# Dilated attention passes that read their tokens as stepped slices of an already transposed tile, in place of transposing raw tokens anew

## The chip, the cores and the metric

The kernel runs on one core of a Trainium2 chip. The metric is the device time of one execution in microseconds; the figure for a kernel is the median of its runs. TensorE multiplies and transposes, ScalarE (ACT), VectorE (DVE) and GpSimd (POOL) work elementwise, and SyncE (SP) issues most DMAs. A matmul of TensorE is preceded by a load of its stationary operand (a weight load, PEld in the profile).

## What is computed

Two groups of tokens, 512 (prompt) and 1024 (sample), each with 1024 features, go through two layers with shared weights. Layer 0 mixes with two kinds of attention, layer 1 with a windowed one, and a routed mixture of experts follows each. The change lies in the dilated half of layer 0's mixer:

```python
h = rms_norm(x, norm_mix[layer])
proj = h @ w_in                       # qa, ka, va (3 groups of 4 heads), qb, kb, vb
A_PATTERNS = ((128, 1), (512, 4), (2048, 16))       # (window, dilation)
for gi, (window, dil) in enumerate(A_PATTERNS):
    o, lse = dilated_window_attn(qa[:, :, gi], ka[:, :, gi], va[:, :, gi], window, dil)
    # to_sub: t.reshape(b, n, dilation, h, dh).transpose(0, 2, 1, 3, 4)
    # tokens of one residue modulo the dilation attend to each other in a band
```

So for dilation 4 and 16 the tokens of a tile of 128 are not neighbours: they are those of one residue modulo a step. The kernel uses steps (1, 1), (4, 4) and (4, 8) for (prompt, sample), and a mask for what is left of 16.

## The kernel before

Tokens are held in NT = 12 tiles of P = 128 (4 of prompt, 8 of sample). `attention_phase` (L390) is called three times in all: "b" (dense, 0 to about 684 us), "a" (dilated, about 684 to 1204 us) and "c" (layer 1). Between them stand `output_phase` and `expert_phase`, which the change does not touch.

For the projections the tokens lie transposed in SBUF, features on partitions and tokens as columns: `hTh` and `hTl`, [128, 8, 1536] of 4-byte values, a high and a low part whose sum is the value. `exact3` (L148) makes one product of three matmuls, high x high, high x low, low x high (L151 to L153). The stationary operand is the slice of 128 tokens, `hTh[:, k, tile_cols(p)]`, and the moving one 384 columns of weights. A projected tile p takes 8 blocks k x 3 = 24 matmuls into `psP`.

The norm is split: the token's 1/rms is not applied to the tokens, but later. `rt` holds the root for each token (applied to V in `evacuate`, L650), and `em` its mean square times EPS (used by `head_roots`, L608). Both are [128, 3, 12]: token within a tile, order (one for each pattern), tile.

Phase "a" runs 6 passes of 12 projected tiles (p = 0 to 71): passes 0 and 1 are pattern a1, 2 and 3 are a4, 4 and 5 are a16; the two passes of a pattern hold two heads' groups each. The order of all work is one list of events (`Work.banded_order`, L269), which every engine walks:
- "P" (p, half): `project`, 12 matmuls; after the second half ScalarE evacuates (`evacuate`, L641 to L650) and squares, GpSimd and VectorE norm and rotate.
- "T": TensorE turns q and k of tile p (L952, L955), ScalarE and VectorE write their high and low parts.
- "S", "R", "V": scores, turned probabilities and the weighted sum of attention, which follow the projection by LAG = 5 tiles. In V's order SP stores the output (L570), with two buffers `osb` in turn.
- "W": split of a quarter of the weights (L627 on ScalarE, L748 on VectorE), loaded by SP.
- "N" (n, half): half a tile of raw tokens. SP loads 256 KB (`load_x`, L524 to L528) with the tokens of the pattern's order (`token_rows`), TensorE transposes four blocks of 128x128 (`turn_x`, L923 to L929), ScalarE casts to `hTh` (L638) and squares `xb` for the mean square (L634), VectorE subtracts to `hTl` (L756), and GpSimd makes `em` and `rt` after the second half (`token_root`, L581 to L589).

`fresh` (L424) says which passes begin a new order of tokens. Phase "b" transposes all 12 tiles once in natural order, and pattern a1 uses them. For a4 and a16 `hTh` and `hTl` are overwritten in place: the 12 tiles "N" of a4 are taken one by one with the projected tiles p = 13 to 24, the 12 of a16 with p = 37 to 48. So the passes 0, 2, 4 and 5 are free of "N" but for their tile 0 in 2 and 4.

`psT` is one double buffer for the results of "N", "T" and "R"; a new one waits until the one before the last was copied out (`room_free`, L911).

Of the kernel before, what the change touches and what calls it, by code (L numbers as in the profile page):

```python
# [7 lines left out]
F32 = mybir.dt.float32  # L8
# [7 lines left out]
P = 128  # L16
SEQ, DEC_SEQ = 512, 1024
TOK = SEQ + DEC_SEQ
NT = TOK // P
# [20 lines left out]
STRIDES = {"b": (1, 1), "c": (1, 1), "a1": (1, 1), "a4": (4, 4), "a16": (4, 8)}  # L40
# [107 lines left out]
def exact3(eng, out, a, b, start, stop):  # L148

    (ah, al), (bh, bl) = a, b  # L150
    eng.matmul(out, ah, bh, start=start, stop=False)  # L151
    eng.matmul(out, ah, bl, start=False, stop=False)  # L152
    return eng.matmul(out, al, bh, start=False, stop=stop)  # L153
# [48 lines left out]
    return first, last - first, base + (first - t + 1) * P  # L202


def token_rows(rows, t, kind):

    g = t >= PT
    stride, first, n, u = STRIDES[kind][g], SEQ * g, (SEQ, DEC_SEQ)[g], t - PT * g
    r, part = divmod(u, n // stride // P)
    return rows[first:first + n].rearrange("(i r) c -> r i c", r=stride)[r, part * P:(part + 1) * P]  # L210


RING, LAG, HELD = 6, 5, 4
# [173 lines left out]
        return u % (self.nq // 2), self.units[u][2][k][0][0] * 3 * P  # L387


def attention_phase(nc, state, name, steps, hT, roots, x_rows, norm_gain, identity, masks, mask0, table, sink=None):  # L390

# [5 lines left out]

    ph = Phase(nc, state)  # L400
    hTh, hTl = hT
    rt, em = roots
    NS = len(steps)
    nq, nkv = steps[0]["nq"], steps[0]["nkv"]
    turns = steps[0]["w"].shape[0] - 1
    nh = nq + nkv
    NC = (nq + 2 * nkv) * HD
# [5 lines left out]
    N = turns * NS  # L413
# [3 lines left out]
    kblk = (pairs + single) * P  # L417
    TC = kblk + nkv * P
    OR = 4 if dense else 2
    XH = {"b": 4, "a": 2, "c": 3}[name]  # L420
    HC = D // 2
    SG = 2 if dense else nq
    order_of = [st["order"] for st in steps for _ in range(turns)]
    fresh = [(order_of[i - 1] if i else None if name != "a" else 0) != order_of[i] for i in range(N)]  # L424
    work = Work(steps, turns, fresh)
    units, groups, events, batch0 = work.units, work.groups, work.events, work.batch0
    UT = len(units)
# [10 lines left out]
    half = ph.sb("half", [P, nh])  # L438
    xb = ph.sb("xb", [P, XH, HC])
    ssx = ph.sb("ssx", [P, 2, 2])  # L440
# [30 lines left out]
    psP = ph.psum("psP", [P, 512])  # L471
# [3 lines left out]
    w_in = [ph.sem(f"w_in{x}") for x in range(RING)]  # L475
    x_in = [ph.sem(f"x_in{x}") for x in range(XH)]
    x_turned, x_high, x_low = ph.sem("x_turned"), ph.sem("x_high"), ph.sem("x_low")
    x_squared, rt_ready = ph.sem("x_squared"), ph.sem("rt_ready")
# [7 lines left out]
    pv_done, o_done, stored = ph.sem("pv_done"), ph.sem("o_done"), [ph.sem(f"stored{x}") for x in range(OR)]  # L486
    dve_order, pool_order, sink_ready = ph.sem("dve_order"), ph.sem("pool_order"), ph.sem("sink_ready")
    half_ready, tally = ph.sem("half_ready"), ph.sem("tally")
    NCONST = 1 + NS + (masks is not None) + (sink is not None)

    def place(p):
# [11 lines left out]
    def tile_cols(p):  # L503
        return slice(p % NT * P, (p % NT + 1) * P)
# [9 lines left out]
    with nc.Block() as block:  # L514

        @block.sync
        def _(sp):
            halves = 2 * len(work.norms)

            def load_x(x):  # L520
                if x >= halves:
                    return
                i, t = work.norms[x // 2]
                if x >= XH:  # L524

                    sp.wait_ge(x_squared, x - XH + 1)
                rows = token_rows(x_rows, t, work.kinds[i])
                sp.dma_start(xb[:, x % XH], rows[:, x % 2 * HC:(x % 2 + 1) * HC]).then_inc(x_in[x % XH], 16)  # L528

            def load_w(q):  # L530
                if q >= N * WQ:
                    return
                if q >= RING:

                    i, quarter = divmod(q - RING, WQ)
                    sp.wait_ge(projected, 2 * (i * NT + NT - 1) + quarter // 2 + 1)
                sp.dma_start(raw_quarter(q), weights(q)).then_inc(w_in[q % RING], 16)

            sp.dma_start(ident, identity).then_inc(ident_in, 16)
            if work.norms[0][0] == 0:  # L540
                load_x(0)
                load_x(1)
            sp.dma_start(gn[:, :], norm_gain).then_inc(gn_in, 16)
            load_w(0)
            load_w(1)
            for x in range(2 if work.norms[0][0] == 0 else 0, XH):
                load_x(x)
            load_w(2)
            load_w(3)
            for s, st in enumerate(steps):  # L550
                sp.dma_start(gains[:, s, :], st["gain"]).then_inc(const_in, 16)
            sp.dma_start(rope[:, :, :, :, :], table).then_inc(const_in, 16)
            if masks is not None:
                sp.dma_start(maskf[:, :], masks).then_inc(const_in, 16)
            if sink is not None:
                sp.dma_start(sinks[:, :], sink).then_inc(const_in, 16)
            ph.clear_previous(sp)
            load_w(4)
            load_w(5)
            for e in events:  # L560
                if e[0] == "N":
                    load_x(2 * e[1] + e[2] + XH)
                if e[0] == "P" and e[1] % NT == NT - 1:
                    for quarter in (0, 1):
                        load_w(e[1] // NT * WQ + RING + 2 * e[2] + quarter)
                if e[0] == "V":
                    for p in tile_done(e[1]):
                        s, turn, t = place(p)
                        sp.wait_ge(o_done, e[1] + 1)
                        sp.dma_start(steps[s]["out"](turn, t), osb[:, p % OR].rearrange("p h c -> p (h c)"))\  # L570
                          .then_inc(stored[p % OR], 16)
            for x in range(OR):
                sp.wait_ge(stored[x], 16 * (total // OR))
# [49 lines left out]
        def _(act):  # L623
# [17 lines left out]
            def evacuate(p):  # L641
                b, (s, _, t) = p % 2, place(p)
                if p >= 2:
                    act.wait_ge(gained, p - 1)
                n = [work.norm_of[i, t] for i in range(p // NT + 1) if (i, t) in work.norm_of]
                if n:
                    act.wait_ge(rt_ready, n[-1] + 1)
                act.wait_ge(projected, 2 * p + 2)
                act.copy(xr[:, b, :], psP[:, 0:nh * HD])
                act.mul(V[:, t, :], psP[:, nh * HD:NC], rt[:, steps[s]["order"], t:t + 1]).then_inc(evacuated, 1)  # L650
# [86 lines left out]
        def _(dve):  # L737
            chain = Chain(dve, dve_order)
            def constants():
                dve.wait_ge(const_in, 16 * NCONST)  # L740
                if sink is not None:
# [163 lines left out]
        def _(pe):  # L905
# [24 lines left out]

            def project(p, half):
                i, t = divmod(p, NT)
                if half == 0 and p:
                    pe.wait_ge(evacuated, p)
                n = [work.norm_of[j, t] for j in range(i + 1) if (j, t) in work.norm_of]
                if n:
                    pe.wait_ge(x_low, 2 * n[-1] + half + 1)
                for k in range(half * KD // 2, (half + 1) * KD // 2):
                    q = i * WQ + k // KW
                    if t == 0 and k % KW == 0:  # L940
                        pe.wait_ge(w_split, q + 1)
                    ins = exact3(pe, psP[:, 0:NC], (hTh[:, k, tile_cols(p)], hTl[:, k, tile_cols(p)]),
                                 (wh[:, q % RING, k % KW, :], wl[:, q % RING, k % KW, :]), k == 0, k == KD - 1)
                ins.then_inc(projected, 1)

# [757 lines left out]
def encoder(nc, a, stop=99):  # L1703
    dram = lambda name, shape: nc.dram_tensor(name, shape, F32, kind="Internal").ap()
    y_rows, x_rows = a["y"], a["x"]
# [11 lines left out]
    with ExitStack() as ctx:  # L1717
        state = {"n": 0, "old": [], "stack": None, "kept": ctx}
# [11 lines left out]
                    expert_phase(nc, state, a["w_gate"][layer], a["w_up"][layer], a["w_down"][layer], a["identity"],  # L1730
                                 lists, idx[:, :], gate[:, :], h_rows, y_rows)

        rt = ctx.enter_context(nc.sbuf_tensor("rt", [P, 3, NT], F32))
        em = ctx.enter_context(nc.sbuf_tensor("em", [P, 3, NT], F32))
        roots = (rt, em)
        with nc.sbuf_tensor("hTh", [P, KD, TOK], F32R) as hTh, nc.sbuf_tensor("hTl", [P, KD, TOK], F32R) as hTl:
            attention_phase(nc, state, "b",
                            [dict(kind="b", nq=B_NQ, nkv=1, order=0, w=a["w_b"], gain=a["gain_b"], out=by_tile(ob, B_NQ))],
                            (hTh, hTl), roots, x_rows, a["gain_mix"][0], a["identity"], None, 0, a["rope_axial"])
            attention_phase(nc, state, "a",  # L1740
                            [dict(kind=k, nq=2, nkv=2, order=s, w=a["w_a"][s], gain=a["gain_a"][s], out=by_residue(s, k))
                             for s, k in enumerate(("a1", "a4", "a16"))],
                            (hTh, hTl), roots, x_rows, a["gain_mix"][0], a["identity"], a["masks"][:, 3 * P:], 3 * P, a["rope_a"])
        moe(0, [(ob, A_OUT)], arec, a["w_out_ab"], x_rows)
        if stop <= 2:
            return
# [56 lines left out]
```

## Time and profile before

| | us |
|---|---|
| median of 3 runs | 4094.46 |
| lowest, highest | 4088.36, 4096.05 |
| profiled execution | 4093.49 |
| its span, first to last instruction | 4091.7 |

| engine | busy us | share of the span |
|---|---|---|
| TensorE, matmuls | 3819.6 | 93% |
| TensorE, weight loads | 3687.8 | 90% |
| VectorE | 2675.3 | 65% |
| ScalarE | 2138.2 | 52% |
| GpSimd | 860.1 | 21% |

The profile is of one execution. Matmuls are pipelined, so the duration of one (0.33 us for 384 columns) is longer than the distance between the starts of two in a row; the distance is what counts. The dilated phase is some 520 of the 4092 us. The granted clock of TensorE was at or near its full level of 2.4 GHz through nearly all of it (0.97 of full as a mean from 684 to 1204 us).

### The profile page before, as it was taken

Reading aid. Unit: us, or ns where it says so; the run is one execution under the profiler, and the core shown is the slowest. Engines: PE = TensorE matmul, PEld = TensorE weight load, DVE = VectorE, ACT = ScalarE, POOL = GpSimd, SP = SyncE. Lnnn points to the kernel's source line nnn. Section 1 sums busy time; section 2 is a strip of 40 time slices with the busy share of each in tenths; the row PEclk is TensorE's granted clock in tenths of the full one; section 3 lists DMA queues with packets and bytes.
Section 4 is the critical chain, followed back from the end, with each engine's and each line's share of the span. In section 5 each row is a group of like instructions: output and inputs, shape, how many; then the busy total and the mean of one; then the engine's idle time right before and its main releaser. Section 6 shows DMA issues by size and latency. Waiting matters only on the chain. (4 is left out here: it accounts for less than half of the span.)

```text
span 4091.7 us, 75095 instructions
## 1 busy us (share of the span) xinstructions
PE 3819.6 (93%) x27032; PEld 3687.8 (90%) x27032; DVE 2675.3 (65%) x5509; ACT 2138.2 (52%) x3992; POOL 860.1 (21%) x1437
## 2 busy tenths in 40 slices
PE   7999998999979779999999969999795999999998
PEld 7988988999978679999999969999785999999998
DVE  5665654666664667777777747776436777777775
ACT  5554544666542245655556545555322565565554
POOL 5122120444420011111111123232000011111110
PEclk9999999999989889999999989999897999999999
DMA  3000001112124377888777721000334788778884
GB/s 104 11 22 7 16 9 50 50 61 68 50 93 154 125 225 252 247 251 249 237 252 246 218 86 42 30 23 14 127 140 159 238 247 255 236 244 252 251 245 127
DMA packets 486184, 584.29 MB, mean 143 GB/s; under 512 B 18128, under 2 KB 439248, under 8 KB 485968
## 3 DMA queue, kind: packets, MB, share of 16 engines
q1 hardware_dynamic: 471632, 531.18, 39.6%
q0 software_dynamic: 14336, 50.34, 5.7%
q8 instruction: 122, 2.00, 0.2%
q14 instruction: 94, 0.77, 0.1%
HBM read 515.25 MB, written 66.21 MB: 142 GB/s over the span
## 5 line engine op out<-in xcount | busy, mean ns | idle before, releaser
L1578 DVE TENSOR_TENSOR wl<-raw,wh 128x2048 fp32r<-128x2048 f32 x384 | 879.2, 2290 | 277.5 <-ACT wh L1533 276.7
L1533 ACT CAST wh<-raw 128x2048 fp32r<-128x2048 f32 x384 | 733.0, 1909 | 25.1 <-DMA raw<-in_w_gate 22.9
L1675 PE MATMUL ps_g<-xT,wh 128*128 128x384 f32 x2048 | 599.7, 359 | 3.2 <-DVE xT L1584 3.2
L1675 PE MATMUL ps_u<-xT,wh 128*128 128x384 f32 x2048 | 594.8, 357 | 0.0
L151 PE MATMUL psP<-wh,hTh 128*128 128x384 f32 (+1 forms) x1344 | 464.3, 345 | 38.9 <-DVE wl L748 33.1
L1677 PE MATMUL ps_g<-xT,wl 128*128 128x192 f32 x2048 | 479.1, 254 | 0.0
L1677 PE MATMUL ps_u<-xT,wl 128*128 128x192 f32 x2048 | 477.1, 253 | 0.0
L153 PE MATMUL psP<-wh,hTl 128*128 128x384 f32 (+1 forms) x1344 | 445.7, 332 | 0.0
L152 PE MATMUL psP<-wl,hTh 128*128 128x384 f32 (+1 forms) x1344 | 445.3, 331 | 0.0
L994 PEld LDWEIGHTS psO<-V,pT 128*128 128x128 f32 x3456 | 425.4, 195 | 17.1 <-issue 9.1
L994 PE MATMUL psO<-V,pT 128*128 128x64 f32 x3456 | 421.4, 275 | 1.9 <-ACT pT L694 1.2
L1677 PEld LDWEIGHTS ps_g<-xT,wl 128*128 128x128 f32 x2048 | 388.8, 192 | 0.0
L1677 PEld LDWEIGHTS ps_u<-xT,wl 128*128 128x128 f32 x2048 | 385.8, 190 | 0.0
L1675 PEld LDWEIGHTS ps_g<-xT,wh 128*128 128x128 f32 x2048 | 378.8, 190 | 3.5 <-issue 3.5
L1675 PEld LDWEIGHTS ps_u<-xT,wh 128*128 128x128 f32 x2048 | 376.1, 189 | 0.0
L682 ACT ACTIVATE prob<-psS,nbias 128x384 f32<-128x384 f32 (+4 forms) x480 | 308.0, 648 | 79.1 <-DVE nbias L820 43.1
L694 ACT COPY pT<-psT 128x512 f32<-128x512 f32 (+2 forms) x348 | 182.8, 539 | 252.1 <-PE psT L978 249.0
L597 POOL TENSOR_TENSOR xg<-xr,gains 128x256 f32<-128x256 f32 (+1 forms) x168 | 130.1, 775 | 813.1 <-ACT V L650 787.1
L151 PEld LDWEIGHTS psP<-wh,hTh 128*128 128x128 f32 x1344 | 256.4, 191 | 45.0 <-issue 31.0
L1497 POOL COPY put_s<-idx 128x1 uint32 (+1 forms) x32 | 5.9, 183 | 1289.3 <-DVE cp L1597 1289.3
L978 PE MATMUL psT<-ident,prob 128*128 128x128 f32 x1728 | 246.1, 276 | 15.4 <-DVE pT L872 4.7
L765 DVE TENSOR_REDUCE ss<-xn 128x4 f32<-128x256 f32 (+1 forms) x168 | 73.6, 438 | 284.4 <-ACT xn L657 284.1
(198 smaller groups left out, 8867.2 us busy)
## 6 DMA issues: line engine op xcount, KB each, us to landing
raw<-in_w_gate SPq DMA_DIRECT2D x128, 1024.0 KB, 5.4
raw<-in_w_up SPq DMA_DIRECT2D x128, 1024.0 KB, 5.2
raw<-in_w_down SPq DMA_DIRECT2D x128, 1024.0 KB, 8.3
xb<-in_x SPq DMA_DIRECT2D x72, 256.0 KB, 2.8
out_y<-yb SPq DMA_DIRECT2D x24, 512.0 KB, 2.7
h_rows<-hb SPq DMA_DIRECT2D x24, 512.0 KB, 3.0
raw<-in_w_a SPq DMA_DIRECT2D x24, 384.0 KB, 4.3
xb<-in_x SPq DMA_DIRECT2D x12, 512.0 KB, 4.7
```

The source lines that it names most:

```text
L151: eng.matmul(out, ah, bh, start=start, stop=False)
L152: eng.matmul(out, ah, bl, start=False, stop=False)
L153: return eng.matmul(out, al, bh, start=False, stop=stop)
L597: pool.tensor_tensor(xg[:, b, :], xr[:, b, :], gains[:, s, :], ALU.mult).then_inc(gained, 1)
L682: ins = act.activation(prob[:, u % 2, c * KC:c * KC + nk * P], psS[:, u % 2, c * 512:c * 512 + nk * P], ACT.Exp, bias=nbias[:, g % 4, x:x ...
L694: act.copy(pT[:, slot, at:at + w], room_of("R", u, k)[:, 0:w]).then_inc(pT_act, 1)
L978: ins = pe.transpose(room_of("R", u, k)[:, x * P:(x + 1) * P], prob[:, u % 2, c * KC + j * P:c * KC + (j + 1) * P], ident)
L994: ins = pe.matmul(psO[:, (off + c) * HD:(off + c + 1) * HD], pT[:, slot, at + x * P:at + (x + 1) * P], V[:, k0 + j, kv * HD:(kv + 1) * HD] ...
L1533: act.copy(wh[:, j % SPL], raw[:, j % RAW]).then_inc(w_high, 1)
L1578: dve.tensor_tensor(wl[:, j % SPL], raw[:, j % RAW], wh[:, j % SPL].bitcast(F32), ALU.subtract)\
L1675: both = lambda **fl: pe.matmul(ps[:, f, 0:2 * CAP], wh[:, j % SPL, k, fs], xT[:, k].rearrange("p h c -> p (h c)"), **fl)
L1677: high = lambda: pe.matmul(ps[:, f, 0:CAP], wl[:, j % SPL, k, fs], xT[:, k, 0, :], start=False, stop=False)
```

## The change

Phase "a" has no "N" events any more. `fresh` is true only for pass 0 of the phases "b" and "c". The stationary operand of a projection is a slice with a step, `hTh[:, k, token_cols(t, kind)]`: for a4 every fourth token of the group, for a16 every fourth (prompt) or eighth (sample). `hTh` and `hTl` stay as phase "b" left them.

The roots `rt` and `em` are put into one array `roots` [128, 3, 12, 2]. Those of order 0 (natural) are stored to DRAM at the start of phase "a", and read back by four DMAs in the order of a4 and a16. SP waits for the store before it issues the loads; this stands after the loads of the first six quarters of weights and before the walk through the events. ScalarE waits for them once for each of the two patterns. The buffer for raw tokens shrinks to one half tile, and none is loaded.

```diff
+def token_place(t, kind):
     g = t >= PT
     stride, first, n, u = STRIDES[kind][g], SEQ * g, (SEQ, DEC_SEQ)[g], t - PT * g
     r, part = divmod(u, n // stride // P)
+    return first, n, stride, r, part
...
+def token_cols(t, kind):
+    first, n, stride, r, part = token_place(t, kind)
+    start = first + r + stride * part * P
+    return slice(start, start + stride * (P - 1) + 1, stride)
...
-    rt, em = roots
+    rt, em = roots[:, :, :, 0], roots[:, :, :, 1]
...
-    XH = {"b": 4, "a": 2, "c": 3}[name]
+    XH = {"b": 4, "a": 1, "c": 3}[name]
...
-    fresh = [(order_of[i - 1] if i else None if name != "a" else 0) != order_of[i] for i in range(N)]
+    fresh = [name != "a" and i == 0 for i in range(N)]
...
+            def reorder_roots():
+                sp.dma_start(roots_out.rearrange("(t p) x -> p t x", p=P), roots[:, 0]).then_inc(roots_stored, 16)
+                sp.wait_ge(roots_stored, 16)
+                for s, st in enumerate(steps[1:], 1):
+                    for first, n in ((0, SEQ), (SEQ, DEC_SEQ)):
+                        stride = STRIDES[st["kind"]][first > 0]
+                        rows = roots_out[first:first + n].rearrange("(u p r) x -> p r u x", p=P, r=stride)
+                        at = roots[:, s, first // P:(first + n) // P].rearrange("p (r u) x -> p r u x", r=stride)
+                        sp.dma_start(at, rows).then_inc(roots_in, 16)
...
             ph.clear_previous(sp)
             load_w(4)
             load_w(5)
+            if NS > 1:
+                reorder_roots()
...
-                n = [work.norm_of[i, t] for i in range(p // NT + 1) if (i, t) in work.norm_of]
-                if n:
-                    act.wait_ge(rt_ready, n[-1] + 1)
+                if (0, t) in work.norm_of:
+                    act.wait_ge(rt_ready, work.norm_of[0, t] + 1)
+                elif p % (NT * turns) == 0 and s:
+                    act.wait_ge(roots_in, 32 * s)
...
                 i, t = divmod(p, NT)
+                toks = token_cols(t, work.kinds[i])
...
-                n = [work.norm_of[j, t] for j in range(i + 1) if (j, t) in work.norm_of]
-                if n:
-                    pe.wait_ge(x_low, 2 * n[-1] + half + 1)
+                if (0, t) in work.norm_of:
+                    pe.wait_ge(x_low, 2 * work.norm_of[0, t] + half + 1)
...
-                    ins = exact3(pe, psP[:, 0:NC], (hTh[:, k, tile_cols(p)], hTl[:, k, tile_cols(p)]),
+                    ins = exact3(pe, psP[:, 0:NC], (hTh[:, k, toks], hTl[:, k, toks]),
```

## Rows read from the trace of the kernel before

**Rows 1.** The page: the span and its first part, busy time by engine.
```profile
span 4091.7 us, 75095 instructions
PE 3819.6 (93%) x27032; PEld 3687.8 (90%) x27032; DVE 2675.3 (65%) x5509; ACT 2138.2 (52%) x3992; POOL 860.1 (21%) x1437
```

**Rows 2.** Stretches (length; busy PE, PEld, DVE, ACT, POOL; clock): passes 1, 3, part of 5.
```profile
767.42:866.68 99.26, 94.14 (x654) 91.29 (x653) 71.36 (x242) 68.84 (x195) 43.53 (x104) 1.00 0.25 76
949.50:1040.19 90.69, 84.68 (x582) 81.53 (x582) 62.39 (x234) 66.14 (x195) 43.84 (x104) 1.00 0.29 87
1124.00:1185.00 61.00, 61.00 (x408) 61.00 (x407) 38.36 (x187) 29.84 (x110) 27.45 (x55) 0.99 0.05 14
```

**Rows 3.** Timeline of ScalarE: start, us, engine, line; last instruction of eleven evacuations.
```profile
719.98 0.37 ACT L650 ACTIVATE V<-psP,rt 128x128 f32<-128x128 f32 x1
...
767.05 0.37 ACT L650 ACTIVATE V<-psP,rt 128x128 f32<-128x128 f32 x1
...
776.97 0.37 ACT L650 ACTIVATE V<-psP,rt 128x128 f32<-128x128 f32 x1
...
866.31 0.37 ACT L650 ACTIVATE V<-psP,rt 128x128 f32<-128x128 f32 x1
...
878.55 0.37 ACT L650 ACTIVATE V<-psP,rt 128x128 f32<-128x128 f32 x1
...
906.91 0.37 ACT L650 ACTIVATE V<-psP,rt 128x128 f32<-128x128 f32 x1
...
949.13 0.37 ACT L650 ACTIVATE V<-psP,rt 128x128 f32<-128x128 f32 x1
...
957.86 0.37 ACT L650 ACTIVATE V<-psP,rt 128x128 f32<-128x128 f32 x1
...
1039.82 0.37 ACT L650 ACTIVATE V<-psP,rt 128x128 f32<-128x128 f32 x1
...
1049.63 0.37 ACT L650 ACTIVATE V<-psP,rt 128x128 f32<-128x128 f32 x1
...
1074.69 0.37 ACT L650 ACTIVATE V<-psP,rt 128x128 f32<-128x128 f32 x1
```

**Rows 4.** Groups by line in the dilated phase (684 to 1204 us).
```profile
L928 PE MATMUL psT<-ident,xb 128*128 128x128 f32 x192 | 29.4, 276 | 6.1 <-ACT pT L694 3.1 <-DVE pT L872 1.5 <-DVE kT L799 1.3
L638 ACT CAST hTh<-psT 128x512 fp32r<-128x512 f32 x48 | 28.1, 586 | 2.0 <-PE psT L928 1.6
L756 DVE TENSOR_TENSOR hTl<-psT,hTh 128x512 fp32r<-128x512 f32 x48 | 32.4, 686 | 2.2 <-ACT hTh L638 1.0
```

**Rows 5.** Timeline at the start of the dilated phase: ScalarE and TensorE.
```profile
694.07 2.13 ACT L627 ACTIVATE wh<-raw,gn 128x384 fp32r<-128x384 f32 x4 [3.58 <-DMA raw<-in_w_a]
...
696.43 0.44 PE L151 MATMUL psP<-wh,hTh 128*128 128x384 f32 x1 [1.57 <-DVE wl L748]
```

**Rows 6.** SP's timeline, and the DMA issues from 1195 to 1240 us.
```profile
729.02 5.96 SPq L570 DMA_DIRECT2D arec<-osb  x2
...
1208.39 3.99 SPq L1136 DMA_DIRECT2D wr<-in_w_router  x1
...
wr<-in_w_router SPq DMA_DIRECT2D x1, 64.0 KB, 13.8
```

**Rows 7.** Timeline of TensorE: projection matmuls in pass 5; weight loads of L994.
```profile
1181.13 0.33 PE L153 MATMUL psP<-wh,hTl 128*128 128x384 f32 x1
...
1184.77 0.34 PE L153 MATMUL psP<-wh,hTl 128*128 128x384 f32 x1
...
857.57 1.48 PEld L994 LDWEIGHTS psO<-V,pT 128*128 128x128 f32 x12
```

**Rows 8.** Groups by line and shape on VectorE, 1200 to 1500 us.
```profile
L1218 DVE TENSOR_TENSOR rp<-rec,rn 128x768 f32<-128x768 f32 x12 | 11.5, 958 | 0.4
L1220 DVE TENSOR_REDUCE ob<-rp 128x256 f32<-128x768 f32 x12 | 12.5, 1038 | 0.4
...
L1207 DVE TENSOR_REDUCE nmin<-rec 128x4 f32<-128x12 f32 x12 | 2.0, 166 | 4.2 <-DMA ob<-ob 4.2
```

More of the change, by code:

```diff
@@ L202, in keys @@
     return first, last - first, base + (first - t + 1) * P
-def token_rows(rows, t, kind):
+def token_place(t, kind):
     g = t >= PT
@@ L209, in token_rows @@
     r, part = divmod(u, n // stride // P)
+    return first, n, stride, r, part
+def token_rows(rows, t, kind):
+    first, n, stride, r, part = token_place(t, kind)
     return rows[first:first + n].rearrange("(i r) c -> r i c", r=stride)[r, part * P:(part + 1) * P]
+def token_cols(t, kind):
+    first, n, stride, r, part = token_place(t, kind)
+    start = first + r + stride * part * P
+    return slice(start, start + stride * (P - 1) + 1, stride)
 RING, LAG, HELD = 6, 5, 4
@@ L387, in spot, with attention_phase @@
         return u % (self.nq // 2), self.units[u][2][k][0][0] * 3 * P
-def attention_phase(nc, state, name, steps, hT, roots, x_rows, norm_gain, identity, masks, mask0, table, sink=None):
+def attention_phase(nc, state, name, steps, hT, roots, x_rows, norm_gain, identity, masks, mask0, table, sink=None, roots_out=None):
     ph = Phase(nc, state)
     hTh, hTl = hT
-    rt, em = roots
+    rt, em = roots[:, :, :, 0], roots[:, :, :, 1]
     NS = len(steps)
@@ L488, in attention_phase @@
     half_ready, tally = ph.sem("half_ready"), ph.sem("tally")
+    roots_stored, roots_in = ph.sem("roots_stored"), ph.sem("roots_in")
     NCONST = 1 + NS + (masks is not None) + (sink is not None)
@@ L539, in _ @@
             sp.dma_start(ident, identity).then_inc(ident_in, 16)
-            if work.norms[0][0] == 0:
+            if work.norms:
                 load_x(0)
@@ L545, in _ @@
             load_w(1)
-            for x in range(2 if work.norms[0][0] == 0 else 0, XH):
+            for x in range(2, XH if work.norms else 0):
                 load_x(x)
@@ L1731, in moe @@
                                  lists, idx[:, :], gate[:, :], h_rows, y_rows)
-        rt = ctx.enter_context(nc.sbuf_tensor("rt", [P, 3, NT], F32))
-        em = ctx.enter_context(nc.sbuf_tensor("em", [P, 3, NT], F32))
-        roots = (rt, em)
+        roots = ctx.enter_context(nc.sbuf_tensor("roots", [P, 3, NT, 2], F32))
         with nc.sbuf_tensor("hTh", [P, KD, TOK], F32R) as hTh, nc.sbuf_tensor("hTl", [P, KD, TOK], F32R) as hTl:
@@ L1742, in encoder @@
                              for s, k in enumerate(("a1", "a4", "a16"))],
-                            (hTh, hTl), roots, x_rows, a["gain_mix"][0], a["identity"], a["masks"][:, 3 * P:], 3 * P, a["rope_a"])
+                            (hTh, hTl), roots, x_rows, a["gain_mix"][0], a["identity"], a["masks"][:, 3 * P:], 3 * P, a["rope_a"],
+                            roots_out=dram("roots_out", (TOK, 2)))
         moe(0, [(ob, A_OUT)], arec, a["w_out_ab"], x_rows)
```

## The prediction

> **What bounds the kernel now.** I read the page first. TensorE is busy 93% of the 4091.7 us span, VectorE 65%, ScalarE 52%, GpSimd 21% [rows 1], so a time saved on TensorE's path is likely a time saved, and work taken from the others counts only where TensorE waits for them. The diff touches only the dilated phase (attention_phase called with name "a"), from about 684 to 1204 us. It has six passes of 12 token tiles: passes 0 and 1 are the plain pattern a1, 2 and 3 are a4, 4 and 5 are a16. A fresh transposition of raw tokens (the events "N") is woven into pass 1 (for a4) and pass 3 (for a16), one tile per projected tile, and nowhere else. That gives a comparison inside the one trace, and the prediction rests on it.
>
> In the view by stretches [rows 2] pass 1 took 99.3 us and pass 3 took 90.7 us, with TensorE idle for some 5 and 6 us; pass 5 has no "N", and in its stretch from 1124 to 1185 us TensorE was busy for 61.00 of 61.00 us at 0.99 of the full granted clock [rows 2]. So a pass with no "N" is bound by TensorE alone, and a pass with it by TensorE plus waits.
>
> **What is removed, first way: by tile times.** Line 650 ends the evacuation of a projected tile, so the distance between two of its instructions is the time of a tile. I compare tiles of the same number t within a pass and with the same kind of attention beside them.
> - Pass 1, tiles 1 to 11, with "N": 866.31 - 776.97 = 89.34 us. The same t without: tiles 1 to 4 of pass 2 (attention of a1 still beside them) 906.91 - 878.55 = 28.36, and tiles 5 to 11 of pass 0, 767.05 - 719.98 = 47.07, in all 75.43. Difference 13.9 us [rows 3].
> - Pass 3, tiles 1 to 11, with "N": 1039.82 - 957.86 = 81.96. Without: tiles 1 to 4 of pass 4, 1074.69 - 1049.63 = 25.06, and tiles 5 to 11 of pass 2, 949.13 - 906.91 = 42.22, in all 67.28. Difference 14.7 us [rows 3].
> - The twelfth "N" of each lies in tile 0 of passes 2 and 4: 878.55 - 866.31 = 12.24 against tile 0 of pass 1, 776.97 - 767.05 = 9.92, is 2.3 us; 1049.63 - 1039.82 = 9.81 against tile 0 of pass 3, 957.86 - 949.13 = 8.73, is 1.1 us [rows 3].
> Sum 13.9 + 14.7 + 2.3 + 1.1 = 32.0 us, or 1.33 us for each of 24 tiles.
>
> **Second way, from below: by instructions.** 192 transposes go (L928). Their busy time of 29.4 us [rows 4] overlaps itself. They can follow each other every 0.12 us (the time of a load, worked out below): 192 x 0.12 = 23 us. The other 9 us are waits: 6.1 us stand before L928 itself [rows 4], the rest where ScalarE and VectorE come late. ScalarE loses the casts (28.1 us) and as many squares, VectorE the subtractions (32.4 us) [rows 4]; GpSimd loses four small instructions for each tile. None of these is a term of its own: their worth is what stands between 23 and 32.0. I take 32.0, as it contains both.
>
> **The start of the phase.** SP issues two 256 KB loads of tokens between the first two and the next two quarters of weights. The third quarter lands at about 694.07, ScalarE having waited 3.58 us for it; TensorE then waits 1.57 us for its low part [rows 5]. Without 512 KB ahead of it the quarter comes sooner than that, and the wait goes: 1.6 us. What is late next is the evacuation of tile 0, which already follows TensorE.
>
> **What is added.** (1) The roots (two values of 4 B for each of 1536 tokens) are stored and read back in four DMAs, in pieces of 8 to 64 B, 1536 of them in the store. The nearest row is the load of w_router, 1024 pieces of 64 B: 3.99 us of SP's time, 13.8 us to landing among 4 MB of other loads [rows 6]. By it the store and the four loads end 30 to 45 us after 695. SP waits for the store with the first output DMA behind it (before at 729.02 [rows 6]); that output may be some 10 us late, but its buffer is wanted again only two tiles on, and the next weights only at the end of pass 0. ScalarE asks for the roots at pass 2, 170 us later. I cost it at nothing; if the cover fails, VectorE's output copy and then TensorE wait once, 0 to 15 us. (2) The evacuation's waits for rt_ready fall away, one wait for roots_in is there for each of two passes, long met: nothing. (3) The roots lie 8 B apart for one-column operands: nothing.
>
> (4) **The strided stationary operand**, the one open price. In passes 2 to 5, 4 x 12 x 8 x 3 = 1152 weight loads take 128 columns that stand 16 B apart (a4, and a16's prompt) or 32 B (a16's sample), instead of 4 B. No load of TensorE in this trace has a step. Its room is known: 21 projection matmuls start between 1181.13 and 1184.77, one each 3.64 / 21 = 0.173 us, say 0.174 [rows 7], which is the time of 384 moving columns; the load of the next one runs beside. Where only 64 columns move, twelve loads take 1.48 us, 0.123 each with the end of the last one in it; I take 0.12 [rows 7]. There the load is the bound, so a plain load needs 0.12 us and may grow to 0.174, 1.45 times, before it costs anything. Below nothing is excluded, since the pitch is then the moving side's. From above the nearest row is VectorE's: L1220 reads 768 values with steps of 256 B in 1038 ns, L1218 the same number without a step in 958 ns, and a small one of 12 costs 166 ns [rows 8]. So a value with a step costs it at most (1038 - 166) / 768 = 1.14 ns, and 128 of them 0.145 us: still under 0.174. I take that row, hence no cost. The other bound is a doubled load: 0.240 - 0.174 = 0.066 us x 1152 = 76 us.
>
> The VectorE row shows an 8% dearer read. The Trainium skill speaks against this change there: "Advanced Engine Details and Errata", SBUF Cachelines, says that two consecutive accesses must fall in the same 16 bytes of SBUF for full speed, and that one access for each line is penalised. By it every load of passes 2 to 5 would slow; the page gives no factor. The trace disagrees for VectorE, and no row shows it for TensorE.
>
> **Sum.** 4093.5 (the profiled execution) - 32.0 - 1.6 = 4059.9; the median of the three runs is 1 us above that execution, so 4060 to 4061. I say 4060.
>
> **The rivals.** Rival 1, slower: the load with a step takes twice as long and the moving side no longer hides it. Price +76 us in passes 2 to 5, where TensorE has no slack [rows 2]: 4060 + 76 = 4136. It is net slower from 33.6 / 1152 = 29 ns more per matmul, a load of 0.203 us, 1.69 times the plain one. For it: TensorE takes a moving column every 0.174 / 384 us = 0.45 ns, a finer beat than VectorE's 1.14, and L1220 reads next to a value that it read three values before. Against it: L1220 at 1.08 times. The Trainium skill's cacheline rule is this case in its hard form.
> Rival 2: a load between 1.45 and 2 times. At 1.7 times, 0.204 us: +0.030 x 1152 = 35 us, 4095, no change to be seen. Its time runs from 4060 to 4136.
> Rival 3: only TensorE's own time comes back and the waits move on to the next late thing (VectorE's chain between a turned tile and its scores): 4093.5 - 23 = 4070. For it: waits tend to be replaced. Against it: the tiles compared above have no "N" and are free of those 9 us.
> Rival 4: the load is slower still, three times or more: 0.360 - 0.174 = 0.186 x 1152 = 214 us, 4274. No row points to it.
> Rival 5: the change doesn't remove what it says, or the roots' detour stalls the phase. "fresh" is false for all passes of "a", so "N" is gone; the stall is bounded by 15 us: 4075.
>
> **How the numbers follow.** Forecast with rivals 3 and 5 (4048 to 4080, the load hidden): 0.74. Rival 2: 0.08. Rival 1: 0.13. Rival 4: 0.05. The range reaches from 4048 (stretches compared may hide another 12 us of shared waits) to 4112, which takes in most of rival 2 and leaves out rivals 1 and 4. A measurement of this kernel can tell about 0.2%, 8 us: faster is below 4086. Faster: 0.74 and a third of rival 2 and a rest, 0.77; same 0.05; slower 0.18.
>
> **What would show it.** L928, L638, L756 and L634 gone from the dilated phase; passes 1 and 3 some 15 us shorter each; the pitch of L151 to L153 in passes 2 to 5 still 0.174 us and their loads under 0.3 us. If the pitch is about 0.24 us there and 0.174 us in passes 0 and 1, rival 1 holds. If the pitch stays and the phase is less than 25 us shorter, rival 3. SP's outputs of the first tiles much later than 729 us with VectorE waiting on stored would be rival 5. The forecast is wrong if the weight load cannot hide under 384 moving columns.

## The result, and the profile after

The changed kernel took 4125.88 us (median of 4 runs, 4124.99 to 4127.67); the kernel before, on the same chip, 4092.41 (median of 4). The ratio is 1.0084, with a 95% interval of 1.0069 to 1.0099: slower by 0.84%, 33 us. I had forecast 4060 and a range of 4048 to 4112. Rival 1 of the prediction, the doubled load at 4136, comes nearest: its mechanism is what the rows below show, at a price 10 us smaller.

The page of the changed kernel, its span and its busy times; the rows of before that answer are [rows 1].

```profile
span 4125.9 us, 74241 instructions
...
PE 3867.5 (94%) x26840; PEld 3743.2 (91%) x26840; DVE 2643.2 (64%) x5461; ACT 2083.1 (50%) x3848; POOL 836.8 (20%) x1341
```

ScalarE and VectorE have less to do (2083.1 us against 2138.2, 2643.2 against 2675.3 [rows 1]), and TensorE, which lost 192 transposes, is busy for 48 us more. The view by stretches says where. These are passes 1 to 5 of the dilated phase (length; busy PE, PEld, DVE, ACT, POOL; granted clock; the last two columns are DMA):

```profile
767.86:853.70 85.84, 82.87 (x566) 81.90 (x566) 56.70 (x220) 44.33 (x129) 30.85 (x60) 1.00 0.09 29
853.70:950.88 97.18, 95.48 (x522) 95.09 (x522) 51.97 (x216) 41.41 (x128) 30.85 (x60) 0.98 0.09 29
950.88:1043.92 93.04, 91.53 (x494) 91.27 (x494) 48.49 (x212) 41.29 (x129) 30.89 (x60) 0.98 0.09 26
1043.92:1135.57 91.65, 90.34 (x480) 90.09 (x480) 47.40 (x212) 39.47 (x129) 30.88 (x60) 1.00 0.09 28
1135.57:1224.68 89.11, 87.37 (x446) 87.12 (x446) 43.96 (x208) 34.89 (x125) 29.91 (x60) 0.98 0.04 10
```

Passes 1 and 3 of before stand in [rows 2]; these are its passes 2, 4 and 5:

```profile
866.68:949.50 82.82, 79.44 (x530) 78.63 (x530) 53.91 (x218) 43.59 (x135) 32.39 (x65) 0.98 0.14 45
...
1040.19:1114.97 74.78, 72.45 (x489) 71.47 (x488) 48.74 (x214) 41.60 (x134) 32.15 (x64) 1.00 0.12 39
1114.97:1185.86 70.89, 68.25 (x447) 67.96 (x446) 43.97 (x208) 34.77 (x125) 29.95 (x60) 0.98 0.06 17
```

Pass 1 fell from 99.26 to 85.84 us: it no longer has its "N". Pass 2 rose from 82.82 to 97.18, pass 4 from 74.78 to 91.65, pass 5 from 70.89 to 89.11, at a granted clock of 0.98 or more in both kernels; TensorE now stands idle for less than 2 us in each of them. Pass 3, which lost its "N", still rose from 90.69 [rows 2] to 93.04.

The weight loads name the cause. Groups of L152's loads in the changed kernel: pass 1 (800 to 850 us, no step), pass 3 (965 to 1010 us, step 4) and pass 5 (1145 to 1195 us, step 4 or 8); the last number ahead of the second bar is the mean in ns.

```profile
L152 PEld LDWEIGHTS psP<-wl,hTh 128*128 128x128 f32 x59 | 11.1, 188 | 0.0
...
L152 PEld LDWEIGHTS psP<-wl,hTh 128*128 128x128 f32 x49 | 16.2, 330 | 0.0
...
L152 PEld LDWEIGHTS psP<-wl,hTh 128*128 128x128 f32 x56 | 18.8, 335 | 0.0
```

And the pitch, the distance between the starts of two matmuls in a row. Matmuls of passes 2 and 5 in the timeline of the changed kernel, 21 and 18 projection matmuls apart:

```profile
907.67 0.40 PE L152 MATMUL psP<-wl,hTh 128*128 128x384 f32 x1
...
912.57 0.40 PE L152 MATMUL psP<-wl,hTh 128*128 128x384 f32 x1
...
1218.49 0.41 PE L153 MATMUL psP<-wh,hTl 128*128 128x384 f32 x1
...
1222.82 0.40 PE L153 MATMUL psP<-wh,hTl 128*128 128x384 f32 x1
```

(912.57 - 907.67) / 21 = 0.233 us with a step of 4, (1222.82 - 1218.49) / 18 = 0.241 us with a step of 8; it was 0.173 before [rows 7]. The duration of a load in the records (188 ns plain) is longer than the 0.12 us at which plain loads can follow each other [rows 7], so durations compare loads with each other, and the pitch gives the price in time. By the pitch a load with a step of 4 takes 0.233 / 0.12 = 1.94 times a plain one.

SP's timeline shows the roots' detour:

```profile
694.87 0.44 SPq L545 DMA_DIRECT2D roots_out<-roots  x1
...
703.84 2.27 SPq L552 DMA_DIRECT2D roots<-roots_out  x4
...
729.46 26.15 SPq L596 DMA_DIRECT2D arec<-osb  x5
```

The store takes 0.44 us to issue, the four loads follow it 9 us later, and the first output goes at 729.46, where it stood at 729.02 before [rows 6].

### The profile page after: what moved, and what is told of

Same layout as the page of the kernel before. It is cut to its first block and busy times, and to the rows that moved or that the text cites. A ratio compares the mean times of both kernels' runs of the same rounds, so it can differ in the third digit from the quotient of the medians.

```text
span 4125.9 us, 74241 instructions
## 1 busy us (share of the span) xinstructions
PE 3867.5 (94%) x26840; PEld 3743.2 (91%) x26840; DVE 2643.2 (64%) x5461; ACT 2083.1 (50%) x3848; POOL 836.8 (20%) x1341
## 5 line engine op out<-in xcount | busy, mean ns | idle before, releaser
L151 PE MATMUL psP<-wh,hTh 128*128 128x384 f32 (+1 forms) x1344 | 491.8, 366 | 33.9 <-DVE wl L775 28.1
L153 PE MATMUL psP<-wh,hTl 128*128 128x384 f32 (+1 forms) x1344 | 471.1, 351 | 0.0
L152 PE MATMUL psP<-wl,hTh 128*128 128x384 f32 (+1 forms) x1344 | 471.0, 350 | 0.0
L151 PEld LDWEIGHTS psP<-wh,hTh 128*128 128x128 f32 x1344 | 312.3, 232 | 39.6 <-issue 20.3
L152 PEld LDWEIGHTS psP<-wl,hTh 128*128 128x128 f32 x1344 | 313.3, 233 | 0.0
L153 PEld LDWEIGHTS psP<-wh,hTl 128*128 128x128 f32 x1344 | 312.4, 232 | 0.0
```

## The experiments

**1. Is the step the whole loss?** The changed kernel, with neighbouring columns in passes 2 to 5, which therefore project the wrong tokens:

```diff
-                toks = token_cols(t, work.kinds[i])
+                toks = tile_cols(p)
```

> The changed kernel, but the projections of passes 2 to 5 read 128 neighbouring columns (tile_cols) as before, so those passes project the wrong tokens; all else, the missing transpositions and the reordered roots too, stays. If the stepped weight load is the whole loss: the pitch of L151 to L153 is 0.174 us in all passes and the time is that of my forecast, 4060 us. If the waits only move on (rival 3): about 4070. If the roots' detour or something else of the change costs: 4075 or more, up to the 4126 of the changed kernel.

Measured: 4060.85 us (median of 4), ratio to before 0.9927 (0.9910 to 0.9943). Its passes 1 to 5:

```profile
767.89:855.32 87.43, 84.47 (x566) 83.50 (x565) 56.75 (x220) 44.32 (x129) 30.82 (x60) 0.98 0.09 28
855.32:936.08 80.76, 76.91 (x522) 76.07 (x522) 52.80 (x216) 41.39 (x129) 30.82 (x60) 1.00 0.10 30
936.08:1013.70 77.62, 74.69 (x494) 73.97 (x494) 49.12 (x212) 41.28 (x129) 30.84 (x60) 0.98 0.10 32
1013.70:1087.24 73.54, 71.23 (x480) 70.57 (x480) 47.35 (x212) 39.54 (x129) 30.88 (x60) 1.00 0.11 35
1087.24:1158.02 70.78, 68.26 (x446) 67.94 (x446) 43.91 (x208) 34.88 (x124) 29.93 (x60) 0.98 0.06 17
```

The step is the whole loss. Everything but the step is worth -32 us by the medians (23 to 37 by the interval of the ratio); against this run the changed kernel's passes 2 to 5 are 370.98 - 302.70 = 68.3 us longer, or 59 ns for each of 1152 matmuls. Rival 5 is out: nothing of the rest costs 15 us. Rival 3 (4070) is out as well: the four runs took 4058.9 to 4062.4 us, and the passes 0 to 5 together are 28.3 us shorter than before, where it gave 23 for everything.

The total agrees with the forecast of 4060 to 1 us, which is closer than its parts. Of the 32.0 us forecast for the transpositions the passes show 28.3, and the start of the phase 1.8 for 1.6. Single passes can't be compared more closely than 1 to 2 us: pass 1 does the same work in this run and in the changed kernel, and took 87.43 us at a granted clock of 0.98 and 85.84 at 1.00.

**2. Which steps cost?** The same kernel with another step in each pass, on the wrong tokens:

```diff
-                toks = token_cols(t, work.kinds[i])
+                step = (1, 1, 2, 3, 4, 12)[i] if name == "a" else 1
+                toks = slice(t, t + step * (P - 1) + 1, step) if step > 1 else tile_cols(p)
```

> The changed kernel, with other steps of the stationary slice: pass 2 reads columns 2 apart (8 B), pass 3 columns 3 apart (12 B), pass 4 columns 4 apart (16 B), pass 5 columns 12 apart (48 B); the tokens of these passes are the wrong ones. Theory A (what counts is whether two loads in a row fall into one piece of 16 B): step 2 hidden, a pitch of 0.174 us; step 3 between, 0.18 to 0.21; steps 4 and 12 alike at 0.235 to 0.24. Theory B (any step other than 1 halves the load): 0.235 in all four passes. Theory C (the cost grows with the step): 0.20, 0.22, 0.235, over 0.26.

One run, 4102.8 us. L152's loads in passes 2, 3, 4 and 5, that is with steps 2, 3, 4 and 12:

```profile
L152 PEld LDWEIGHTS psP<-wl,hTh 128*128 128x128 f32 x61 | 11.9, 195 | 0.0
...
L152 PEld LDWEIGHTS psP<-wl,hTh 128*128 128x128 f32 x61 | 15.5, 254 | 0.0
...
L152 PEld LDWEIGHTS psP<-wl,hTh 128*128 128x128 f32 x47 | 15.4, 329 | 0.0
...
L152 PEld LDWEIGHTS psP<-wl,hTh 128*128 128x128 f32 x52 | 19.3, 370 | 0.0
```

The pitch with steps of 3 and 12, from matmuls that stand 21 apart:

```profile
994.84 0.34 PE L152 MATMUL psP<-wl,hTh 128*128 128x384 f32 x1
...
998.59 0.34 PE L152 MATMUL psP<-wl,hTh 128*128 128x384 f32 x1
...
1152.36 0.44 PE L152 MATMUL psP<-wl,hTh 128*128 128x384 f32 x1
...
1158.04 0.45 PE L152 MATMUL psP<-wl,hTh 128*128 128x384 f32 x1
```

Against 188 ns without a step, the load takes 195, 254, 329 and 370 ns. The pitch is 3.75 / 21 = 0.179 us at step 3 and 5.68 / 21 = 0.270 at step 12; the medians of the distances within a pass are 0.176 at step 2, 0.179 at 3, 0.233 at 4 and 0.267 at 12. So theory B is wrong, and theory A right up to 4: a step of two columns is nearly free, three is dearer but still hidden beneath 384 moving columns, four is not hidden. Step 12 was expected at 0.24 by A; 0.270 is 0.030 more, which A does not explain.

**3. What lies between 4 and 12?** The same with `(1, 1, 5, 7, 8, 10)`.

> As the run with steps 2, 3, 4 and 12, with steps of 5, 7, 8 and 10 columns (20, 28, 32 and 40 B) in passes 2 to 5, wrong tokens. If each load of a column from a new 16 B piece costs the same: 0.235 us in all four, and the 0.271 of step 12 is something of its own. If the cost grows with the distance: from 0.236 in pass 2 to about 0.26 in pass 5. If even steps that are multiples of four columns meet a bank twice: step 8 at 0.240 stands above 5, 7 and 10.

L152's loads with steps 5, 7, 8 and 10:

```profile
L152 PEld LDWEIGHTS psP<-wl,hTh 128*128 128x128 f32 x60 | 19.4, 324 | 0.0
...
L152 PEld LDWEIGHTS psP<-wl,hTh 128*128 128x128 f32 x80 | 26.6, 332 | 0.0
...
L152 PEld LDWEIGHTS psP<-wl,hTh 128*128 128x128 f32 x76 | 25.8, 340 | 0.0
...
L152 PEld LDWEIGHTS psP<-wl,hTh 128*128 128x128 f32 x79 | 26.5, 335 | 0.0
```

One run, 4121.85 us. The loads take 324, 332, 340 and 335 ns, the pitches (medians of the distances within a pass) are 0.229, 0.237, 0.243 and 0.240 us. From 4 to 10 columns the cost is all but flat; step 8 is the highest, but by 5 ns of 340, too little to single it out. The first theory holds for these steps within some 5%, and step 12 stays apart, unexplained.

**4. Does the load hide behind a longer matmul?** The changed kernel, each projection matmul of the dilated phase moving 512 columns (128 of them of the next block, so that the projections are wrong):

```diff
-                    ins = exact3(pe, psP[:, 0:NC], (hTh[:, k, toks], hTl[:, k, toks]),
-                                 (wh[:, q % RING, k % KW, :], wl[:, q % RING, k % KW, :]), k == 0, k == KD - 1)
+                    if name == "a":
+                        ins = exact3(pe, psP[:, 0:512], (hTh[:, k, toks], hTl[:, k, toks]),
+                                     (wh[:, q % RING].rearrange("p k c -> p (k c)")[:, 0:512],
+                                      wl[:, q % RING].rearrange("p k c -> p (k c)")[:, 0:512]), k == 0, k == KD - 1)
...
```

> The changed kernel, with every projection matmul of the dilated phase moving 512 columns in place of 384 (the 128 more are weights of the next block, so the projections are wrong). If a load runs beside the matmul before it and only the longer of the two counts: plain passes 0 and 1 go from a pitch of 0.174 to about 0.233 us, and the stepped passes 2 to 5 stay at 0.235 to 0.24, so that the step costs nearly nothing there: the time is 4126 + 576 x 0.059 = 4160. If a stepped load adds to the matmul in place of hiding (a shared read path): passes 2 to 5 go to about 0.30 us and the time to 4126 + 34 + 1152 x 0.06 = 4229.

One run, 4164.0 us. Matmuls 21 apart in pass 1 (no step) and pass 3 (step 4):

```profile
853.55 0.40 PE L152 MATMUL psP<-wl,hTh 128*128 128x512 f32 x1
...
858.36 0.39 PE L152 MATMUL psP<-wl,hTh 128*128 128x512 f32 x1
...
1000.23 0.40 PE L152 MATMUL psP<-wl,hTh 128*128 128x512 f32 x1
...
1005.16 0.40 PE L152 MATMUL psP<-wl,hTh 128*128 128x512 f32 x1
```

4.81 / 21 = 0.229 us without a step and 4.93 / 21 = 0.235 with one (0.246 with the steps of 8 in the samples of passes 4 and 5). A third more moving columns cost the stepped passes nearly nothing (0.235 for 0.233, 0.246 for 0.241), and the plain ones 0.055 us a matmul. That is the first of the two expectations, 4160 us against 4229: the load runs beside the matmul ahead of it, and the longer of the two counts.

**5. Was the VectorE row a bad witness?** The changed kernel with one extra copy of 4 x 128 columns on VectorE and one on ScalarE for each tile, into a scratch tile that nobody reads:

```diff
...
+                        act.copy(xb[:, 1].rearrange("p (k c) -> p k c", c=P),
+                                 hTh[:, 0:4, slice(0, step * (P - 1) + 1, step)].bitcast(F32)).then_inc(read_act, 1)
...
+                    dve.tensor_copy(xb[:, 0].rearrange("p (k c) -> p k c", c=P),
+                                    hTl[:, 0:4, slice(0, step * (P - 1) + 1, step)].bitcast(F32)).then_inc(read_dve, 1)
```

> The changed kernel with one more copy on VectorE (from hTl) and one on ScalarE (from hTh) for each projected tile, four blocks of 128 columns into a scratch tile, with steps of 1, 2, 3, 4, 8 and 10 columns in passes 0 to 5; the copies' results are not used. It asks whether the VectorE row of my sum (1.14 ns for a value with a step) misjudged the memory or only TensorE. If every engine pays for a new piece of 16 B as TensorE's load did (1.9 ns a value): the copies of 512 values take 0.6 to 0.7 us at steps 1 and 2 and about 1.1 to 1.2 us from step 4 on. If VectorE and ScalarE read slowly enough to hide it: 0.6 to 0.7 us at every step. The row of L1220 itself then came from reading each piece again at once, if the first holds.

One run, 4129.35 us. The groups by line and shape, for steps 1, 2, 3 and 4 (steps 8 and 10: 1179 and 1158 ns on ScalarE, 669 and 640 on VectorE):

```profile
L759 ACT COPY xb<-hTh 128x512 f32<-128x512 f32 x10 | 6.2, 617 | 0.0
L928 DVE COPY xb<-hTl 128x512 f32<-128x512 f32 x10 | 4.2, 419 | 0.0
...
L759 ACT COPY xb<-hTh 128x512 f32<-128x512 f32 x9 | 5.8, 646 | 0.0
L928 DVE COPY xb<-hTl 128x512 f32<-128x512 f32 x9 | 3.8, 420 | 0.0
...
L759 ACT COPY xb<-hTh 128x512 f32<-128x512 f32 x9 | 8.0, 888 | 0.0
L928 DVE COPY xb<-hTl 128x512 f32<-128x512 f32 x9 | 4.5, 501 | 0.0
...
L759 ACT COPY xb<-hTh 128x512 f32<-128x512 f32 x10 | 11.2, 1118 | 0.0
L928 DVE COPY xb<-hTl 128x512 f32<-128x512 f32 x10 | 6.2, 617 | 0.0
```

All three engines pay, from step 3 on, and most of the price is there at step 4: ScalarE goes from 617 to 1118 ns, (1118 - 617) / 512 = 0.98 ns more for each value; TensorE's load in the changed kernel pays (330 - 188) / 128 = 1.11 ns by the durations and (0.233 - 0.12) / 128 = 0.88 ns by the pitch; VectorE only (617 - 419) / 512 = 0.39 ns. ScalarE did what the first expectation says; VectorE stayed within 0.6 to 0.7 us, as the second has it, but only because its plain copy, at 0.419, is faster than expected. The steps change with the pass here, and from pass 2 on TensorE reads with a step too; that this slows the others can be left out, since the unchanged operations of both engines took the same in every pass (L685 417 or 418 ns, L799 419 or 420).

Why did L1220 not show it? The trace of before has the same operation, TENSOR_REDUCE, on values without a step (683.8 to 1204 us):

```profile
L765 DVE TENSOR_REDUCE ss<-xn 128x4 f32<-128x256 f32 x72 | 30.2, 420 | 141.2 <-ACT xn L657 140.8
```

With the 166 ns of a small operation [rows 8] taken off, a plain reduction spends (420 - 166) / 256 = 0.99 ns on a value and L1220, with its step, 1.14; a copy with a step of 4 columns spends (617 - 166) / 512 = 0.88 and a plain one 0.49. The reduction is slow enough to hide most of what the copy pays. This is worked out from rows of different lengths; no run has one reduction with and without a step.

**6. The other part alone.** The kernel before with only the roots' detour: both rounds of transpositions stay, the squares on ScalarE and GpSimd's four instructions go, and the first raw tiles are loaded behind the weights.

```diff
...
-                    to_square.append(e[1:])
+                    if name != "a":
+                        to_square.append(e[1:])
...
-                if e[0] == "N" and e[2] == 1:
+                if e[0] == "N" and e[2] == 1 and name != "a":
                     token_root(e[1])
...
```

> The kernel before with one part of the change: the roots of a4 and a16 come by the DMA detour and the raw tiles are no longer squared, but both rounds of transpositions stay and no slice has a step; the first raw tiles are loaded behind all weights. If the transpositions cost by TensorE's own time alone, and the 9 us of waits came from the squares on ScalarE: 4092.6 - 9 - 1.6 = 4082. If the waits come from the casts and subtractions, which stay: 4090 to 4091. If the detour costs: above 4092.

Measured: 4086.14 us (median of 12), the kernel before on the same chip 4087.50 (median of 17), ratio 0.9991 (0.9982 to 0.9999). Its passes 1 and 3:

```profile
768.31:867.19 98.88, 93.96 (x654) 91.29 (x654) 70.33 (x242) 56.07 (x151) 30.90 (x60) 1.00 0.27 83
948.79:1040.73 91.94, 86.16 (x582) 83.03 (x582) 62.35 (x234) 53.07 (x151) 30.91 (x60) 0.98 0.31 89
```

ScalarE is 13 us less busy in each (56.07 against 68.84, 53.07 against 66.14 [rows 2]), and the passes take 98.88 and 91.94 us, where they took 99.26 and 90.69. TensorE stood idle for 4.9 and 5.8 us in them, against 5.1 and 6.0 before. The whole is shorter by 0.4 to 7 us by the interval, with some 1.6 us forecast for the start, so the squares were worth little, and not the 9 us of the first expectation. The waits around the transpositions are not theirs; that they come from the casts and subtractions was the other expectation, and was not tried by itself.

**7. A version between the two.** Step 2 is free, so order the tokens once for a4 and read a16 from that order: the four prompt tiles are the same, and a sample tile (residue r of 8) is every second column of the 256 that hold residue r mod 4.

```diff
+    if kind == "a16" and t >= PT:
+        r = t - PT
+        start = SEQ + r % 4 * 2 * P + r // 4
+        return slice(start, start + 2 * (P - 1) + 1, 2)
+    return slice(t * P, (t + 1) * P)
...
-    fresh = [name != "a" and i == 0 for i in range(N)]
+    fresh = [i == (turns if name == "a" else 0) for i in range(N)]
...
```

> A full kernel between the two. The tokens of a4 are transposed anew, woven into pass 1 as before; those of a16 are then taken from a4's order, where its prompt tiles are the same and its sample tiles are slices with a step of 2 columns (8 B). The roots come by the DMA detour and no raw tile is squared; the first raw tiles are loaded behind all weights. If a step of 2 is hidden (pitch 0.178 us against 0.174): before 4092.6, less the 14.7 + 1.1 us of the second round of transpositions, less 1.6 at the start, plus 384 x 0.004 = 1.5, less 0 to 4 for the missing squares: 4073 to 4077. If a stepped slice costs what it did in the changed kernel (+0.066 us): 4100.

Measured, with the reference's full computation: 4072.65 us (median of 5), ratio to before 0.9957 (0.9944 to 0.9970). Passes 1 to 5, and L152's loads in pass 5 (step 2 in the sample):

```profile
767.19:867.57 100.38, 95.50 (x654) 92.89 (x653) 70.27 (x242) 56.00 (x150) 30.82 (x60) 0.98 0.26 82
867.57:947.62 80.05, 77.76 (x530) 77.06 (x530) 53.15 (x218) 42.38 (x131) 30.88 (x60) 1.00 0.10 32
947.62:1023.43 75.81, 73.08 (x495) 72.36 (x494) 48.91 (x212) 41.29 (x129) 30.84 (x60) 1.00 0.11 33
1023.43:1098.61 75.18, 72.90 (x480) 72.25 (x480) 47.59 (x212) 39.57 (x129) 30.87 (x60) 0.98 0.11 34
1098.61:1169.63 71.02, 68.53 (x446) 68.15 (x446) 44.04 (x208) 34.91 (x124) 29.91 (x60) 0.98 0.06 17
```

```profile
L152 PEld LDWEIGHTS psP<-wl,hTh 128*128 128x128 f32 x57 | 11.1, 195 | 0.0
```

Pass 3 is 75.81 us, 14.9 less than before; passes 4 and 5 stand within 2 us of the run of experiment 1, and pass 1 keeps its "N" at 100.4. The load is 195 ns and hidden. The forecast was 16 to 20 us less than before; the ratio gives 18 (12 to 23), the two medians on that chip, 4072.65 against 4087.50, give 15. The version is faster than the kernel before and than the changed one, by 0.4% and by some 1.2% (from the ratios of both to before).

## Why the prediction was wrong

**Right: what goes.** By tile times I had 13.9 us for pass 1, 14.7 for pass 3, 2.3 and 1.1 for the tiles 0 of passes 2 and 4. Experiment 1 gave 99.26 - 87.43 = 11.8 for pass 1 (13.4 in the changed kernel), 90.69 - 77.62 = 13.1 for pass 3 (14.9 in experiment 7), 2.1 for pass 2, 1.2 for pass 4, with 0.1 for pass 5 in all 28.3 for my 32.0, and the whole as 4092.8 - 4060.9 = 32 us against my 33.6. Passes 1 and 3 of experiment 1 had a granted clock of 0.98, the two in brackets 1.00 like those of before; the same work at the lower clock took 1.6 and 1.8 us longer. Comparing like tiles inside one trace was the good half of this work; counting instructions alone would have given 23. That the total came out within 1 us of 4060 is in part luck.

**Too strong: "a pass with no "N" is bound by TensorE alone".** The stretch of 61.00 of 61.00 us leaves out the first tiles of pass 5. Over the whole passes 4 and 5 of before TensorE was idle for 2.3 and 2.6 us. This cushioned the step a little: in passes 2 to 5 the idle time of TensorE went from 11.6 us (experiment 1) to 6.3 (the changed kernel).

**Right: the start and the detour.** The evacuation of tile 0 came 699.57 - 685.49 = 14.1 us after SP's first DMA of the phase (before 699.12 - 683.80 = 15.3): 1.2 us saved, against 1.6. The store of the roots landed in 9 us, not in the 14 of w_router's row, the loads in some 2, and no wait shows: the first output went at 729.46 us, and pass 0 took 67.9 us in both kernels.

**Wrong: step (4), the stepped load.** Its frame was right. The room of 0.174 us over 0.12, that the load costs nothing up to 1.45 times, and that only the excess counts, all held (experiments 2 and 4). The part of it that failed is the value that I put in: "From above the nearest row is VectorE's", 0.145 us for 128 values. The load took 0.233 to 0.241 us, twice the plain one, so it showed past the 0.174 us of the moving columns, and a term that I put at nothing cost 68.3 us. I took another engine's price for the same memory, and did not ask whether that engine was slow enough to hide it. A plain reduction spends 0.99 ns on a value and L1220 1.14; a TensorE load has 0.12 / 128 = 0.94 ns, and it pays 0.88 ns more once the values lie 16 B apart. The 8% that I read was off as well, since L1218 is another operation; against the plain reduction L1220 is 15% dearer for each value. I also had the doubled load as the other bound and gave it 0.13; its price, 76 us, was near the 68.3 measured in the passes. The difference is that a step of 4 gives 0.233 where I had 0.240, and that some 5 us went into time that TensorE had stood idle.

The rule that I quoted, from the Trainium skill's "Advanced Engine Details and Errata", SBUF Cachelines, asks for at least two accesses in a row in the same 16 bytes for full speed. The runs agree up to a step of 10. Step 2, two to a piece, cost 7 ns of 188; step 3, four in three pieces, 66; step 4, each in its own, 141. The 370 ns of step 12 the rule doesn't explain. I had it beside the row and let the row of another engine outweigh it. Where the page gave no factor, the honest range was from 1 to 2 times with both ends likely, and it would have held the result.

## What to carry to other kernels

In these runs a slice with a step as the stationary operand was all but free at two 4-byte columns and about doubled the load from four on; it costs the excess of that load over the matmul that runs beside it, here 59 ns each next to 384 moving columns, and 6 ns (step 4) to 17 ns (step 8) next to 512. If data must be read in several strided orders, and one of them leaves the others a step of two at most, store it in that one, as experiment 7 does. And bound the cost of an access on one engine by a row of another only if that row is faster for each value than the engine that you price; a slower row hides what you look for.

## What the runs showed of the hardware

- TensorE's load of 128 columns of 4 bytes, mean duration by step: 188 ns at 1, 195 at 2, 254 at 3, 329 at 4, 324 at 5, 332 at 7, 340 at 8, 335 at 10, 370 at 12. The last stands above the plateau and is not explained here.
- The same threshold on ScalarE (617, 646, 888, 1118 ns for 512 values at steps 1 to 4) and on VectorE (419, 420, 501, 617): the excess for a value at step 4 is 0.98 ns on ScalarE, 0.39 on VectorE, and 0.88 (pitch) or 1.11 (duration) for TensorE's load.
- 512 moving columns go every 0.229 us, 384 every 0.173: a load with a step of 4, at 0.235, is all but covered by the first; with a step of 8 the pitch is 0.246.
- Freeing ScalarE of 13 us of work in a pass of 99 changed the pass by 0.4 us: TensorE's idle time in it stayed at 4.9 us (5.1 before).
